# Attention weights normalised in place and turned by a transpose, with the matmuls of two heads issued alternately

## What is computed

```python
# first kind: causal, q and k normalised and rotated
s = einsum('bhqd,bhnd->bhqn', q, k) * scale
s = where(kpos <= qpos, s, NEG)
p = softmax(s, axis=-1)
out = einsum('bhqn,bhnd->bhqd', p, v)
# second kind: all keys within a window, with a learned bias
s = einsum('bhcd,bhrckd->bhcrk', q_row, k_win) * scale + bias
p = softmax(s, axis=-1)
out = einsum('bhcrk,bhrckd->bhcd', p, v_win)
```

## Time and profile before

| | |
|---|---|
| time, median of 3 runs | 2128.6 us (2124.53 to 2132.08) |
| the profiled execution | 2127.8 us, of which 2126.0 us from its first to its last instruction |
| TensorE busy | 2063.8 us, 97% |
| VectorE, ScalarE, GpSimd busy | 1298.3, 1087.7, 316.8 us |
| mean share of the 16 DMA engines | about half, 169 GB/s |
| mean granted clock of TensorE | 0.989 |
| a chunk's `w_hi` on ScalarE, `w_lo` on VectorE | 1.90 us, 2.33 us |

### The profile page before, as it was taken

One profiled execution on the slowest core, in us unless ns is written; L12 is line 12 of the kernel. 1 busy time (PEld: TensorE's weight loads), 2 busy tenths in 40 slices (PEclk: granted clock), 3 DMA queues, 4 the chain that ended last, 5 costly groups with the idle time before them and its releaser, 6 DMA issues.

```text
span 2126.0 us, 36714 instructions
## 1 busy us (share of the span) xinstructions
PE 2063.8 (97%) x14600; PEld 1917.8 (90%) x14600; DVE 1298.3 (61%) x1472; ACT 1087.7 (51%) x1312; POOL 316.8 (15%) x239
## 2 busy tenths in 40 slices
PE   6999999999999999999999999999998999999997
PEld 5999989899889999898999899999997989999996
DVE  6555655655665566467556645567775545567775
ACT  5445555544554465545446443356655443355554
POOL 3000331300010033033004003230004103220001
PEclk9999999999999999999999999999998999999998
DMA  6554534454455454345555434544543434544451
GB/s 244 196 178 178 179 127 152 161 193 179 159 189 187 178 179 170 128 159 203 188 184 184 147 139 147 191 180 177 192 178 132 162 134 145 183 162 176 182 193 60
DMA packets 53287, 360.04 MB, mean 169 GB/s; under 512 B 6321, under 2 KB 7729, under 8 KB 10545
## 3 DMA queue, kind: packets, MB, share of 16 engines
q1 hardware_dynamic: 49248, 350.01, 45.9%
q10 hardware_dynamic: 3328, 4.20, 0.7%
q0 software_dynamic: 592, 4.19, 0.5%
HBM read 353.14 MB, written 1.05 MB: 167 GB/s over the span
## 4 chain that ended last, share of the span: by engine, by line
PE 60%; issue 30%; POOL 5%; ACT 2%; DVE 2%; DMA 1%; SPq 0%; POOLq 0%; DVEq 0%; ACTq 0%
PE up_two L1394 7%; PE gate_two L1359 7%; PE gate_two L1360 7%; PE gate_two L1361 7%; PE gate_two L1394 6%; PE bank L1359 5%; PE bank L1361 5%; PE bank L1360 5%; PE up_two L1396 4%; PE gate_two L1396 3%; POOL br_parts L405 2%; POOL in_parts L405 2%; PE bank L1468 1%; PE up_two L1482 1%; PE up_two L1498 1%
## 5 line engine op out<-in xcount | busy, mean ns | idle before, releaser
L921 DVE TENSOR_TENSOR w_lo<-raw,w_hi 128x2048 fp32r<-128x2048 f32 x330 | 767.1, 2325 | 345.5 <-ACT w_hi L545 345.3
L545 ACT ACTIVATE w_hi<-raw 128x2048 fp32r<-128x2048 f32 x330 | 628.3, 1904 | 72.8 <-PE bank L1361 68.7
L1360 PE MATMUL bank<-hid_hi,w_lo 128*128 128x256 f32 x960 | 271.6, 283 | 0.0
L1359 PE MATMUL bank<-hid_lo,w_hi 128*128 128x256 f32 x960 | 271.5, 283 | 0.0
L1361 PE MATMUL bank<-hid_hi,w_hi 128*128 128x256 f32 x960 | 271.5, 283 | 0.0
L1394 PE MATMUL gate_two<-in_parts,w_hi 128*128 128x512 f32 x640 | 229.1, 400 | 6.6 <-POOL in_parts L405 6.6
L1359 PE MATMUL gate_two<-br_parts,w_hi 128*128 128x256 f32 x768 | 223.8, 291 | 11.6 <-POOL br_parts L405 5.7
L1394 PE MATMUL up_two<-in_parts,w_hi 128*128 128x512 f32 x640 | 227.8, 399 | 0.4 <-DVE w_lo L921 0.4
L1360 PE MATMUL gate_two<-br_parts,w_lo 128*128 128x256 f32 x768 | 219.7, 286 | 0.0
L1361 PE MATMUL gate_two<-br_parts,w_hi 128*128 128x256 f32 x768 | 219.7, 286 | 0.0
L1359 PEld LDWEIGHTS bank<-hid_lo,w_hi 128*128 128x128 f32 x960 | 183.8, 191 | 3.0
(11 more groups left out here) (257 smaller groups left out, 4517.5 us busy)
## 6 DMA issues: line engine op xcount, KB each, us to landing
raw<-stream SPq DMA_DIRECT2D x330, 1024.0 KB, 4.8
area<-rpb POOLq DMA_DIRECT2D x2, 1536.0 KB, 7.7
softT<-area ACTq DMA_DIRECT2D x32, 64.0 KB, 4.4
konst<-consts SPq DMA_DIRECT2D x1, 1344.0 KB, 13.4
x<-xT SPq DMA_DIRECT2D x4, 256.0 KB, 4.0
area<-area ACTq DMA_DIRECT2D x8, 128.0 KB, 4.9
ret_turn<-area ACTq DMA_DIRECT2D x8, 128.0 KB, 4.7
result<-x SPq DMA_DIRECT2D x4, 256.0 KB, 2.0
```

What stands on the lines that cost most here:

```text
L545: act.activation(w_hi[:, s, :], raw[:, s, :], ACT.Copy).then_inc(hi_ready[s], 1)
L921: dve.tensor_tensor(w_lo[:, s, :], raw[:, s, :], w_hi[:, s, :].bitcast(F32), ALU.subtract).then_inc(lo_ready[s], 1)
L1359: pe.matmul(out, whi, xlo, start=start, stop=False, skip_group_check=True)
L1360: pe.matmul(out, wlo, xhi, start=False, stop=False, skip_group_check=True)
```

## The change

`weigh` is gone. `softmax_weights` scales `soft` in place, by one tensor_scalar for each block of queries, and no longer waits for the turning of the head before. `turn_weights` calls `pe.transpose` with the identity. `scores` and `weigh_values` take a pair of heads j (heads 2j and 2j+1) and issue their matmuls alternately, one of the lower half and one of the upper. Scores of a pair are made at every other step, when the first of its heads was due, and wait for `max_ready` of the pair before; values of a pair are made when the second of its heads was due. Within a step the order is now values, turning, scores.

```diff
@@ softmax_weights (VectorE)
-                if h >= 1:
-                    dve.wait_ge(p_turned.sem, here.at(p_turned, h))
-                dve.tensor_tensor(weigh[:, :, :], ident.unsqueeze(1).broadcast_to([P, TT, P]),
-                                  stat[:, b, 6:8].unsqueeze(2).broadcast_to([P, TT, P]), ALU.mult
-                                  ).then_inc(weigh_ready.sem, 1)
+                for a in range(TT):
+                    part = soft[:, b, a, 0:keys[a]]
+                    e = dve.tensor_scalar(part, part, stat[:, b, 6 + a:7 + a], None, ALU.mult)
+                e.then_inc(weigh_ready.sem, 1)
@@ scores
-            def scores(here, h, keys, q_ready):
-                q_ready()
-                rows = slice(HEAD_DIM * (h % 2), HEAD_DIM * (h % 2 + 1))
+            def scores(here, j, keys):
+
+                if j >= 1:
+                    pe.wait_ge(max_ready.sem, here.at(max_ready, 2 * j))
                 for a in range(TT):
-                    e = pe.matmul(banks[2 + h % 2][:, a, 0:keys[a]], qk[rows, h // 2, a * P:(a + 1) * P],
-                                  qk[rows, HALVES + h // 2, 0:keys[a]], start=True, stop=True, skip_group_check=True)
-                e.then_inc(scored.sem, 1)
+                    for half in range(2):
+                        rows = slice(HEAD_DIM * half, HEAD_DIM * (half + 1))
+                        e = pe.matmul(banks[2 + half][:, a, 0:keys[a]], qk[rows, j, a * P:(a + 1) * P],
+                                      qk[rows, HALVES + j, 0:keys[a]], start=True, stop=True, skip_group_check=True)
+                        if a == TT - 1:
+                            e.then_inc(scored.sem, 1)
@@ turn_weights
-                            e = pe.matmul(turned[:, at:at + P], soft[:, h % 2, a, k * P:(k + 1) * P], weigh[:, a, :],
-                                          start=True, stop=True, skip_group_check=True)
+                            e = pe.transpose(turned[:, at:at + P], soft[:, h % 2, a, k * P:(k + 1) * P], ident)
@@ weigh_values
-            def weigh_values(here, h, keys):
-                pe.wait_ge(pT_ready.sem, here.at(pT_ready, h + 1))
-                j = h // 2
+            def weigh_values(here, j, keys):
+
+                pe.wait_ge(pT_ready.sem, here.at(pT_ready, 2 * j + 2))
                 if j >= 1:
                     pe.wait_ge(att_ready.sem, here.at(att_ready, j))
-                rows = slice(HEAD_DIM * (h % 2), HEAD_DIM * (h % 2 + 1))
-                weights = flat(softT[:, h % 2, :, :])
                 at = 0
                 for k in range(TT):
 
                     n = P * sum(k * P < keys[a] for a in range(TT))
-                    e = pe.matmul(banks[7][rows, j % 2, T - n:T], v_tok[:, k, h * HEAD_DIM:(h + 1) * HEAD_DIM],
-                                  weights[:, at:at + n], start=k == 0, stop=k == TT - 1, skip_group_check=True)
+                    for half in range(2):
+                        rows = slice(HEAD_DIM * half, HEAD_DIM * (half + 1))
+                        h = 2 * j + half
+                        e = pe.matmul(banks[7][rows, j % 2, T - n:T], v_tok[:, k, h * HEAD_DIM:(h + 1) * HEAD_DIM],
+                                      flat(softT[:, half, :, :])[:, at:at + n], start=k == 0, stop=k == TT - 1,
+                                      skip_group_check=True)
+                        if k == TT - 1:
+                            e.then_inc(pv_done.sem, 1)
                     at += n
-                e.then_inc(pv_done.sem, 1)
@@ the steps of the first kind (the second has 8, 6, 5 for 10, 8, 7, and waits for mix_evac)
-                    if 0 <= m - 7 < HEADS:
-                        scores(here, m - 7, CAUSAL_KEYS, lambda: pe.wait_ge(k_normed.sem, here.at(k_normed, 2)))
+                    if m >= 10 and m % 2 == 0 and (m - 10) // 2 < HALVES:
+                        weigh_values(here, (m - 10) // 2, CAUSAL_KEYS)
                     if 0 <= m - 8 < HEADS:
                         turn_weights(here, m - 8, CAUSAL_KEYS)
-                    if 0 <= m - 9 < HEADS:
-                        weigh_values(here, m - 9, CAUSAL_KEYS)
+                    if m % 2 == 1 and 0 <= (m - 7) // 2 < HALVES:
+                        pe.wait_ge(k_normed.sem, here.at(k_normed, 2))
+                        scores(here, (m - 7) // 2, CAUSAL_KEYS)
```

More of the change, by code:

```diff
@@ L166, in hybrid_and_neighbourhood_kernel @@
         k_cols = sb("k_cols", [P, TT, 2 * P])
-        weigh = sb("weigh", [P, TT, P])
         stat = sb("stat", [P, 2, 8])
@@ L1034, in softmax_scores, with softmax_weights @@
                 e.then_inc(nmax_ready.sem, 1)
-            def softmax_weights(here, h):
+            def softmax_weights(here, h, keys):
                 b = h % 2
@@ L1131, in _ @@
                     if 0 <= m - 7 < HEADS:
-                        softmax_weights(here, m - 7)
+                        softmax_weights(here, m - 7, CAUSAL_KEYS)
                     if m == 18:
@@ L1276, in _ @@
                     if 0 <= m - 5 < HEADS:
-                        softmax_weights(here, m - 5)
+                        softmax_weights(here, m - 5, ALL_KEYS)
                     if m == 35:
@@ L1700, in _ @@
                         features(m, two(bank), br_hi, br_lo, DT)
-                    if 0 <= m - 5 < HEADS:
-                        scores(here, m - 5, ALL_KEYS, lambda: pe.wait_ge(mix_evac.sem, here.at(mix_evac, 4)))
+                    if m >= 8 and m % 2 == 0 and (m - 8) // 2 < HALVES:
+                        weigh_values(here, (m - 8) // 2, ALL_KEYS)
                     if 0 <= m - 6 < HEADS:
                         turn_weights(here, m - 6, ALL_KEYS)
-                    if 0 <= m - 7 < HEADS:
-                        weigh_values(here, m - 7, ALL_KEYS)
+                    if m % 2 == 1 and 0 <= (m - 5) // 2 < HALVES:
+                        pe.wait_ge(mix_evac.sem, here.at(mix_evac, 4))
+                        scores(here, (m - 5) // 2, ALL_KEYS)
                     if 0 <= m - 15 < RET_HEADS:
```

## The result

Before 2128.8 us (median of 4 runs, 2124.5 to 2132.1), after 2079.9 us (4 runs, 2078.8 to 2083.0): the ratio is 0.977, 95% interval 0.975 to 0.979. The sign came as forecast, and so did two of the three terms of the gain; the third, two heads side by side, was priced 14 us too low. The time lies 14 us under the forecast of 2094 and 4 us under the low end of the range.

The account below looks back on a forecast made before the run. TensorE, busy for 97% of the span, was taken to bound the kernel. Savings of 12.7 (transposes), 11.7 (shape changes) and 10 us (halves side by side) sum to 34.4: 2128.6 - 34.4 = 2094 us, range 2084 to 2107.

Parts of the forecast that it names:

- (a): Turning of the attention weights on TensorE: one-pass transposes replace two-pass f32 matmuls, 12.7 us less.
- (b): Attention steps on TensorE: fewer changes of array shape, 16 instead of 32 a layer, 11.7 us less.
- (c): Scores and weighted values of two heads on halves of TensorE's array: partial overlap, 10 us less.
- rival 1: Scores and values of a head pair overlap perfectly on the array's halves: 2087 us, down to 2080; chance 0.20.
- (d): VectorE in attention: `weigh` goes, two tensor_scalar come, +0.3 us a head, all hidden, so 0 us.
- (e): Attention's softmax ring through ScalarE and VectorE: margins shrink to 2.5 and some 3.6 us but stay, so 0 us.
- Rival 2: Scores and values of a head pair do not overlap, f32 passes stay in line: 2104 us; chance 0.15.
- rival 3: Going from half to half of the array costs a change each time, no overlap: 2120 to 2122 us; chance 0.06.
- Rival 4: The ring at turning's wait for `weigh_ready` becomes the bound, slower: 2170 us at twice the reckoned ring; chance 0.03.
- Rival 5: TensorE's clock falls to its lower level, slower: about 2390 us if all of attention is at it; chance 0.02.
- Rival 6: In the turning, an f32 transpose is issued as two passes, so transposes bring nothing: 2107 us; chance 0.04.
- The pool branch: GpSimd's branch keeps its own time; TensorE reaches its matmuls about 1.5 us sooner, 4 us are left: 0 us.

Follow-up runs that it names:

- a_alone: The kernel before with only weights scaled in place and turned by transposes, heads, order and shape changes kept: 2114.5 us, ratio 0.991-0.995.
- split_pairs: The changed kernel with a step's transposes put mid-scores or mid-values, after the first matmul of both halves, so halves still stand together: 2090.2 us.
- split_halves: The changed kernel with a step's transposes put between the two halves' matmuls of scores or values, so halves cannot overlap there: 2107.2 us.
- delay4: The changed kernel with four unread, serial 128x256 f32 copies on VectorE ahead of each head's normalising: 2091.8 us, ratio 0.981-0.984.
- delay9: The changed kernel with nine unread, serial 128x256 f32 copies on VectorE ahead of each head's normalising: 2124.4 us, ratio 0.996-1.000.

## Why the prediction was right and where it failed

**(a) Transposes.** Priced 12.7, measured 13.7 added alone and 13.2 taken out of the change. Right. Some of the surplus is at the entry: a_alone's four transposes take 0.59 us between scores and values, 0.44 for the passes and 0.15 for the change of shape, where the eight passes of the earlier trace rows had 0.89 and 0.20; term (a) had counted the passes alone.

**(b) Changes of shape.** Priced 11.7. split_pairs brings three quarters of them back (48 of 64) and costs 8.4 for 8.2 expected. Right.

**(c) Halves side by side.** Priced 10, measured 23.8 by split_halves against split_pairs, scaled from three pairs to four. This is the term that failed, and its 14 us are the whole miss. I had named bounds of 0 and 17.3 and written that a lower end still, four pass times for a pair, would add 7: 24.3, which is what happened. The step that failed is "If the load of B waits for the start of A's second pass". It took a rule of order from rows in which every load and every pass used the full array, and carried it to halves. The earlier trace rows could show only that a load waits for the pass ahead on the same rows and columns; they couldn't show what it does when the half is free. The step before it, that a matmul's two passes stay together and so A and B queue as A A B B, fell too: even when the code issues them in that order the passes run in pairs. An even step of the full stage runs from 1188.23 to 1195.49, 7.26 us, where 7.8 had been worked out, and the odd one after it to 1203.03, 7.54 for 8.0. The remark on reading operands was off too: two streams of values ask for 2 x 256 columns in 0.216 us, one fp32r stream for 256 in 0.12, so together they ask for 11% more and not for less. They run side by side all the same. With (c) at 24.3 the same sum gives 2128.6 - 12.7 - 11.7 - 24.3 = 2079.9.

**The range.** It was built from the case 2087 of rival 1 less 3 us, and left out that rival's own lower end, 2080, with its seven microseconds. The bound that counted was in the text, with its price, and not in the range.

**(d) VectorE.** Priced at +0.3 a head between 0 and 0.66, hidden. The groups by form show what two tensor_scalar cost:

```profile
L1043 DVE TENSOR_SCALAR soft<-soft,stat 128x256 f32<-128x256 f32 x48 | 16.2, 365 | 0.6
L1043 DVE TENSOR_SCALAR soft<-soft,stat 128x128 f32<-128x128 f32 x16 | 4.6, 288 | 0.6
```

A pair of the longer form takes 0.62 us where `weigh` took 0.42: 0.2 more, and no wait of TensorE comes of it. Right.

**(e) Waits.** No wait arose, as forecast, but the margin was misread. I worked out 2.5 and 3.6 us from one step. From the end of the first tensor_scalar of a head to the start of its turning, head by head, the changed kernel has 2.29, 2.29, 5.18, 2.83, 4.07, 3.21, 4.07, 3.21 in the first kind and 3.06, **0.36**, 1.99, 1.79, 3.40, 3.12, 4.16, 3.12 in the second; where TensorE does wait for the second tensor_scalar, in delay4, this distance is 0.32, so that much is no room. Head 1 of the second kind stands at the very edge. Its step, ScalarE's time line:

```profile
1160.50 2.20 ACTq L640 DMA_DIRECT2D area<-area  x2
1162.82 0.63 ACT L829 ACTIVATE area<-area 128x512 f32<-128x512 f32 x1 [2.35 <-issue]
1163.36 0.58 ACT L648 ACTIVATE softT<-up_two 128x512 f32<-128x512 f32 x1
1163.84 0.50 ACT L629 ACTIVATE soft<-soft,stat 128x256 f32<-128x256 f32 x1
```

then VectorE and TensorE:

```profile
1164.95 0.17 DVE L1039 RECIPROCAL stat<-stat 128x2 f32<-128x2 f32 x1 [3.56 <-ACT soft L629]
1165.16 0.62 DVE L1043 TENSOR_SCALAR soft<-soft,stat 128x256 f32<-128x256 f32 x2
```

```profile
1165.87 0.62 PE L1484 MATMUL up_two<-konst,soft 128*128 128x128 f32 x4
```

ScalarE issues two DMAs (2.20 us of its queue) and an exponential of the retention decays ahead of the copy and the softmax. Only the steps in which that work stands have so little room, and I had read a step without it. In this kernel it cost nothing, and with 1.28 us more on VectorE, in delay4, it stalled TensorE by 0.4 us (and not by all of it, since ScalarE's two DMA issues took 1.38 us there for 2.20 here).

**Rivals.** Rival 1 at its lower end is what happened. Rival 2 (2104) is out, since splitting three of the four pairs costs 17.9 us, and rival 3 (2120) too: going from half to half costs 7 ns. Rival 4 didn't occur and needs some 2.6 us more on VectorE for each head. Rival 5 didn't: the clock is 1.00 in all four stages; it fell there only in delay9, behind the stalls of rival 4. Rival 6 is out: 112 instructions for L1484, 0.109 us apart.

**The pool branch** has GpSimd's end at 283.3 and its matmuls (L1607) at 286.21: 2.9 us left, where I had reckoned 4, since TensorE came 3.1 us sooner and not 1.5; not late.

**"All later stages keep their lengths"** holds for their sum (+0.7 us) and not for each: the five stretches outside attention changed by -0.4, +3.0, -0.5, -4.1 and +2.8 us. The second has a mean clock of 1.00 before and 0.99 after, the fourth 0.97 and 0.98, which goes with their signs; the fifth shows 0.98 in both. Differences of 3 to 5 us between kernels can come from there.

## What to carry to other kernels

Work on a half of TensorE's array costs the full time of the array; two such jobs of the same shape that use different rows or different columns cost together what one costs, if they stand next to each other. That held here for two f32 matmuls to a half, alternating or one half after the other. Put f32 turnings on transposes (one pass, not two), and group work of the same shape, since each change of shape cost 0.15 to 0.2 us here. When a bound of an unknown cost stands in the sum's text, it belongs in the range, and a margin is to be read at the step with the most on the slow engine, not at a typical one.

## What the hardware showed that I had not expected

- Two f32 streams on halves of the array run without slowing each other: eight passes of 256 columns of two halves take 1.01 to 1.07 us, as four of one half do, for halves by rows and by columns alike.
- A matmul of the other half is let through ahead of one issued before it: its first pass starts 13 ns after the first half's first, though the first half's second matmul was issued ahead of it. Whether that is a look ahead in one queue, a queue for each half or a new order made before the array, and how far it reaches, stays open; so does what two row halves do that write the same bank, which wasn't tried.
- VectorE's f32 copies of 128x256 take 0.29 us each alone and 0.6 while GpSimd runs tensor_tensors of the same size (2.54 against 1.28 us for four). The Trainium skill (GPSIMD Engine Reference, 1. Specifications) says that GpSimd's SBUF interfaces are shared with VectorE, with contention where a VectorE instruction has two SBUF inputs or runs in a mode that uses two ports. This trace shows the slowdown, a factor of two for this pair; a copy has one input, and which mode it ran in the trace doesn't show.
- The time lost to the lower clock level between the stages varies by 13 us over nine kernels with the same work there (20.8 to 33.6, one execution each, by the means of the table). Executions of one and the same kernel vary as much: 0.985 to 0.990 in 29 of the kernel before is 21 to 32 us.
